# A layer's first RMS norm moved into the stage of the mixer's input projection

## What is computed

```python
def _rms(x, g):
    xf = x.astype(jnp.float32)
    y = xf * lax.rsqrt(jnp.mean(xf * xf, axis=-1, keepdims=True) + EPS)
    return (y * g.astype(jnp.float32)).astype(x.dtype)

def _layer(x, cond, p, ck, cv, cstate):
    mod = jax.nn.silu(cond) @ p['w_mod'] + p['b_mod']
    sh1, sc1, g1, sh2, sc2, g2 = jnp.split(mod, N_MOD, axis=-1)
    h = _rms(x, p['norm1']) * (1.0 + sc1) + sh1
    out, ctx = _token_mixers(h, p, ck, cv, cstate)
    x = x + g1 * out
    ...
```

## Time and profile before

| | |
|---|---|
| median of 3 runs | 5839.04 us (5838.94 to 5841.78) |
| the profiled execution | 5846.38 us, its span 5844.6 us |
| TensorE busy (matmul) | 5424.8 us, 93% of the span |
| TensorE weight loads | 5213.8 us, 89% |
| VectorE | 3252.5 us, 56% |
| ScalarE | 2191.8 us, 38% |
| GpSimd | 2133.7 us, 37% |
| mean granted TensorE clock | 0.966 of 2.4 GHz |

### The profile page before, as it was taken

How to read it: one execution, slowest core, us unless ns; L and a number is a source line. 1 busy time by engine, 2 the same in 40 slices (tenths; PEclk the granted TensorE clock), 3 DMA queues, 4 the chain that set the end, 5 groups by cost and what they waited for, 6 DMA issues and landing times. The chain is left out here.

```text
span 5844.6 us, 118044 instructions
## 1 busy us (share of the span) xinstructions
PE 5424.8 (93%) x47828; PEld 5213.8 (89%) x47828; DVE 3252.5 (56%) x6038; ACT 2191.8 (38%) x2761; POOL 2133.7 (37%) x968
## 2 busy tenths in 40 slices
PE   7977888999999999999989688889999999999999
PEld 3856788999999999999977577889999999999998
DVE  5545648646654156666644564775556522666665
ACT  4433322555555422222233432235555563222221
POOL 0001222656656533343300012236555654433332
PEclk8989999999999999999999899999999999999999
DMA  6100112455555654545411001225555556455443
GB/s 247 58 25 11 62 55 85 143 170 172 178 168 171 210 193 161 169 164 171 142 63 52 17 5 61 87 92 164 168 172 167 180 164 228 166 173 172 162 168 108
DMA packets 303870, 777.73 MB, mean 133 GB/s; under 512 B 23596, under 2 KB 109100, under 8 KB 299368
## 3 DMA queue, kind: packets, MB, share of 16 engines
q1 hardware_dynamic: 303464, 771.94, 39.2%
HBM read 586.52 MB, written 185.34 MB: 132 GB/s over the span
## 5 line engine op out<-in xcount | busy, mean ns | idle before, releaser
L2169 POOL TENSOR_TENSOR ex_v_lo<-ex_v_raw,ex_v_hi 128x1024 fp32r<-128x1024 f32 x256 | 692.1, 2725 | 1071.1 <-ACT ex_v_hi L2075 1071.1
L344 PE MATMUL ex_ps<-tk_h_hi,tk_u_hi 128*128 128x320 f32 x4096 | 968.4, 318 | 43.6 <-POOL tk_u_lo L2157 35.1
L344 PE MATMUL ex_ps<-tk_h_hi,tk_u_lo 128*128 128x320 f32 x4096 | 940.9, 311 | 26.8 <-issue 26.8
L2157 POOL TENSOR_TENSOR tk_u_lo<-tk_u_raw,tk_u_hi 128x1024 fp32r<-128x1024 f32 x256 | 643.4, 2514 | 882.0 <-ACT tk_u_hi L2045 881.7
L344 PE MATMUL ex_ps<-ex_wa_hi,ex_v_hi 128*128 128x320 f32 x4096 | 935.2, 310 | 18.8 <-issue 18.8
L344 PE MATMUL ex_ps<-tk_h_lo,tk_u_hi 128*128 128x320 f32 x4096 | 938.8, 311 | 0.0
L344 PE MATMUL ex_ps<-ex_wa_lo,ex_v_hi 128*128 128x320 f32 x4096 | 934.6, 309 | 0.0
L344 PE MATMUL ex_ps<-ex_wa_hi,ex_v_lo 128*128 128x320 f32 x4096 | 934.5, 309 | 0.0
L2329 DVE TENSOR_TENSOR ex_y<-ex_y,ex_ps 128x640 f32<-128x640 f32 x496 | 405.9, 818 | 671.3 <-PE ex_ps L344 666.5
L344 PEld LDWEIGHTS ex_ps<-tk_h_hi,tk_u_hi 128*128 128x128 f32 x4096 | 682.7, 190 | 45.6 <-POOL tk_u_lo L2157 36.0
L344 PEld LDWEIGHTS ex_ps<-tk_h_hi,tk_u_lo 128*128 128x128 f32 x4096 | 690.8, 189 | 27.5 <-issue 27.5
(11 more groups left out here) (323 smaller groups left out, 7783.2 us busy)
## 6 DMA issues: line engine op xcount, KB each, us to landing
tk_u_raw<-in_expert_u SPq DMA_DIRECT2D x256, 512.0 KB, 4.4
ex_v_raw<-in_expert_v SPq DMA_DIRECT2D x256, 512.0 KB, 3.5
act_spill<-tk_act_e SPq DMA_DIRECT2D x256, 320.0 KB, 2.3
grid_scratch<-tk_grid SPq DMA_DIRECT2D x160, 512.0 KB, 5.7
ex_g<-grid_scratch SPq DMA_DIRECT2D x64, 1280.0 KB, 10.5
x<-in_w_mod_rows SPq DMA_DIRECT2D x192, 256.0 KB, 4.8
ex_a<-act_spill SPq DMA_DIRECT2D x32, 1280.0 KB, 6.3
x<-act_spill SPq DMA_DIRECT2D x32, 1280.0 KB, 6.3
```

The lines of the kernel that those rows point to most:

```text
L344: ins = nc.tensor.matmul(out[:, q, 0:HALF], a, b[:, q * HALF:(q + 1) * HALF], start=(first and n == 0), stop=(last and n == 2))
L2157: nc.gpsimd.tensor_tensor(u_lo[:, at % 2], u_raw[:, at % 3], u_hi[:, at % 2].bitcast(F32), ALU.subtract).then_inc(e["u_split"], 1)
L2169: nc.gpsimd.tensor_tensor(v_lo[h][:, k], v_raw[:, k], v_hi[h][:, k].bitcast(F32), ALU.subtract).then_inc(e["v_split"], 1)
```

## The change

The call of rms_modulate for the first norm goes; its instructions are written into the streams of mixer_input's stage, with the same arithmetic. Its buffers are now parts of rk (h, total and the reciprocal) and of side (sums, wide and the target of the fillers), which the stage uses later for other things. One stage is left where there were two.

On SP nothing is edited: the requests of weights 0 and 1, the constants and the spill of x are the stage's first instructions. On ACT high(0) stands between the squares and the root, high(1) behind the root, then come the eight high parts, then high(2). On DVE low(0) stands between the additions and the mean, low(1) between the reciprocal and the scaling loop, low(2) behind it. On PE the fillers beside the squares stay and those in the scaling loop go; blocks 0 and 1 are made there in first_blocks: in step n PE waits for low part n of the norm, multiplies kb = n for block 0, and kb = n - 3 (BEHIND) for block 1. Block 2 and all later ones are made as before.

```diff
--- before.py
+++ after.py
@@ -350,7 +350,7 @@
 
     order = [Z_AD, Z_WD] + [Z_RKV + 4 + b for b in range(4)] + [Z_RKV + 8 + b for b in range(4)] + \
             [Z_RKV + b for b in range(4)] + [Z_K, 0, 1, 2, 3, Z_V, Z_GD]
-    N = len(order)
+    N, BEHIND = len(order), 3
     FIRST = {name: order.index(n) for name, n in (("k", Z_RKV + 4), ("v", Z_RKV + 8), ("r", Z_RKV), ("qk", Z_K))}
     z, rk = s.z, s.rkv
     value, kmod, kk = s.x[:, 4:8, :], (s.mix[:, 4:8, :], s.x[:, 0:4, :]), s.mix[:, 0:4, :]
@@ -384,11 +384,14 @@
         wide_k, wide_q = z[0:10, Z_V, :], z[0:10, Z_AD, :]
         ps = mem.enter_context(nc.psum_tensor("mi_ps", [P, 2, 2, 512], F32))
         side = mem.enter_context(nc.psum_tensor("mi_side", [P, 2, 2, 512], F32))
+        h, total, inv = rk[:, 0:3, :], rk[:, 3, :], rk[:, 4, 0:TILES]
+        sums, idle, wide = side[:, 0, 0, :], side[:, 0, 1, :], side[:, 1]
 
         names = ["w_in0", "w_in1", "rate_in", "sel_in", "x_out", "hi", "low", "done", "out", "small", "wd_tanh", "rate_done",
                  "rate_tanh", "rate_a", "rate_c", "running", "scanned", "kmod", "conv", "kk_sq", "kk_summed", "kk_ms", "kk_sqrt",
                  "kk_root", "kk_wide", "kk", "kka", "y", "y_summed", "bonus", "bonus_out", "v_turned", "v_taken", "qk_sq",
-                 "qk_summed", "qk_ms", "qk_sqrt", "qk_root", "qk_wide", "qk", "chain"]
+                 "qk_summed", "qk_ms", "qk_sqrt", "qk_root", "qk_wide", "qk", "chain", "x_sq", "x_added", "x_summed", "x_ms", "x_root",
+                 "x_inverse", "x_wide", "x_scaled", "x_high", "x_low"]
         with stage(nc, *["mi_" + n for n in names]) as (block, *sems):
             e = dict(zip(names, sems))
             w_in = (e["w_in0"], e["w_in1"])
@@ -430,11 +433,36 @@
             def _(pe):
                 mm, tr = nc.tensor.matmul, nc.tensor.transpose
 
+                def normed():
+                    for kb in range(KB):
+                        pe.wait_ge(e["x_sq"], kb + 1)
+                        mm(idle[:, 0:HALF], s.ones[:], s.x[:, kb, 0:HALF], start=True, stop=True)
+                    pe.wait_ge(e["x_added"], KB - 1)
+                    for m in range(TILES):
+                        last = mm(sums[:, m:m + 1], total[:, m * P:(m + 1) * P], s.ones[:, 0:1], start=True, stop=True)
+                    last.then_inc(e["x_summed"], 1)
+                    pe.wait_ge(e["x_inverse"], 1)
+                    for m in range(TILES):
+                        out = wide[:, 0, 0:P] if m == 0 else wide[:, 1, (m - 1) * P:m * P]
+                        last = mm(out, inv[:, m:m + 1].broadcast_to([P, P]), s.ident[:], start=True, stop=True)
+                    last.then_inc(e["x_wide"], 1)
+
+                def first_blocks():
+                    pe.wait_ge(e["low"], 2)
+                    for n in range(KB + BEHIND):
+                        if n < KB:
+                            pe.wait_ge(e["x_low"], n + 1)
+                        for u, kb in ((0, n), (1, n - BEHIND)):
+                            if 0 <= kb < KB:
+                                last = matmul_split(nc, ps[:, u], w_hi[:, u, kb], w_lo[:, u, kb], hi[:, kb], lo[:, kb],
+                                                    kb == 0, kb == KB - 1)
+                                if kb == KB - 1:
+                                    last.then_inc(e["done"], 1)
+
                 def project_block(n):
                     u = n % 2
                     pe.wait_ge(e["low"], n + 1)
-                    if n >= 2:
-                        pe.wait_ge(e["out"], n - 1)
+                    pe.wait_ge(e["out"], n - 1)
                     for kb in range(KB):
                         last = matmul_split(nc, ps[:, u], w_hi[:, u, kb], w_lo[:, u, kb], hi[:, kb], lo[:, kb],
                                             kb == 0, kb == KB - 1)
@@ -522,8 +550,11 @@
                         pe.wait_ge(e["qk"], b - 1)
                     widened(side[:, 1 - b % 2], wide_q, root_q, b, 5).then_inc(e["qk_wide"], 1)
 
+                normed()
+                first_blocks()
                 for n in range(N):
-                    project_block(n)
+                    if n >= 2:
+                        project_block(n)
                     if 2 <= n < 10:
                         rates((n - 2) // 4, (n - 2) % 4)
                     if n == 9:
@@ -551,6 +582,12 @@
                         act.wait_ge(e["done"], n - 1)
                     nc.scalar.activation(w_hi[:, n % 2], raw[:, n % 2], ACT.Copy).then_inc(e["hi"], 1)
 
+                def high_part(kb):
+                    act.wait_ge(e["x_scaled"], kb + 1)
+                    for c, a, b in SEGMENTS:
+                        last = nc.scalar.activation(hi[:, kb, a:b], h[:, kb % 3, a:b], ACT.Identity, bias=s.mod[:, kb, c:c + 1])
+                    last.then_inc(e["x_high"], 1)
+
                 def evacuate(n):
                     act.wait_ge(e["done"], n + 1)
                     new = ps[:, n % 2, :, 0:HALF]
@@ -591,11 +628,20 @@
                     act.wait_ge(e["v_turned"], m + 1)
                     nc.scalar.activation(s.v_tok[:, m, :], side[:, 1 - m % 2, 0, :], ACT.Copy).then_inc(e["v_taken"], 1)
 
+                for kb in range(KB):
+                    if kb >= 3:
+                        act.wait_ge(e["x_added"], max(1, kb - 3))
+                    nc.scalar.activation(h[:, kb % 3], s.x[:, kb], ACT.Square).then_inc(e["x_sq"], 1)
                 high(0)
+                act.wait_ge(e["x_ms"], 1)
+                nc.scalar.activation(inv, inv, ACT.Sqrt).then_inc(e["x_root"], 1)
                 high(1)
+                for kb in range(KB):
+                    high_part(kb)
+                high(2)
                 for n in range(N):
                     evacuate(n)
-                    if n + 2 < N:
+                    if 3 <= n + 2 < N:
                         high(n + 2)
                     if n == 1:
                         act.wait_ge(e["out"], 2)
@@ -640,6 +686,21 @@
                     v.tensor_tensor(w_lo[:, n % 2], raw[:, n % 2], w_hi[:, n % 2].bitcast(F32),
                                     ALU.subtract).then_inc(e["low"], 1)
 
+                def scaled(kb):
+                    if kb >= 3:
+                        dve.wait_ge(e["x_low"], kb - 2)
+                    for c, a, b in SEGMENTS:
+                        last = v.scalar_tensor_tensor(h[:, kb % 3, a:b], s.x[:, kb, a:b], s.gain1[:, kb, c:c + 1],
+                                                      wide[:, c, 0:b - a], ALU.mult, ALU.mult)
+                    last.then_inc(e["x_scaled"], 1)
+
+                def low_part(kb):
+                    dve.wait_ge(e["x_high"], kb + 1)
+                    for c, a, b in SEGMENTS:
+                        last = v.scalar_tensor_tensor(lo[:, kb, a:b], h[:, kb % 3, a:b], s.mod[:, kb, c:c + 1],
+                                                      hi[:, kb, a:b].bitcast(F32), ALU.add, ALU.subtract)
+                    last.then_inc(e["x_low"], 1)
+
                 def shifted(zn, j):
                     src, dst = z[:, zn, :], conv_out[zn]
                     for _, a, c in SEGMENTS:
@@ -651,13 +712,28 @@
                 v.tensor_scalar(half0[:, 0:8], s.pvs("a0"), 0.5, None, ALU.mult)
                 v.tensor_scalar(one_ka[:], s.pvs("k_a"), -1.0, 1.0, ALU.mult, ALU.add)
                 v.tensor_scalar(half0[:, 8:16], s.pvs("w0"), 0.5, None, ALU.mult).then_inc(e["small"], 1)
+                for kb in range(1, KB):
+                    dve.wait_ge(e["x_sq"], kb + 1)
+                    v.tensor_tensor(total, h[:, 0] if kb == 1 else total, h[:, kb % 3], ALU.add).then_inc(e["x_added"], 1)
+                    dve.wait_ge(e["x_added"], kb)
                 low(0)
+                dve.wait_ge(e["x_summed"], 1)
+                v.tensor_scalar(inv, sums[:, 0:TILES], 1.0 / D, EPS, ALU.mult, ALU.add).then_inc(e["x_ms"], 1)
+                dve.wait_ge(e["x_root"], 1)
+                v.reciprocal(inv, inv).then_inc(e["x_inverse"], 1)
                 low(1)
+                dve.wait_ge(e["x_wide"], 1)
+                for kb in range(KB):
+                    scaled(kb)
+                    if kb:
+                        low_part(kb - 1)
+                low_part(KB - 1)
+                low(2)
                 for n in range(N):
                     if order[n] in conv_out:
                         dve.wait_ge(e["out"], n + 1)
                         at = link.mark(shifted(order[n], 0))
-                    if n + 2 < N:
+                    if 3 <= n + 2 < N:
                         low(n + 2)
                     if order[n] in conv_out:
                         dve.wait_ge(e["chain"], at)
@@ -2414,7 +2490,6 @@
                 s.rkv = mixers.enter_context(nc.sbuf_tensor("rk", [P, KB, T], F32))
                 with nc.sbuf_tensor("cum", [P, KB, CHUNKS, CHUNK + 1], F32) as cum:
                     with nc.sbuf_tensor("h1_hi", [P, KB, T], F32R) as hi, nc.sbuf_tensor("h1_lo", [P, KB, T], F32R) as lo:
```

(1 more changed line is left out.)

## The result

| | before | after |
|---|---|---|
| median | 5840.41 us (5838.94 to 5843.8, 4 runs) | 5770.34 us (5768.04 to 5781.65, 4 runs) |
| the profiled execution, its span | 5846.38 us, 5844.6 us | 5781.65 us, 5779.5 us |
| mean granted TensorE clock | 0.966 | 0.968 |

The spans differ by 65.1 us. The whole document is about the other half: the two stretches that the change edits give what was forecast, and the rest comes from a place that the change doesn't touch.

What follows compares the result with a forecast made beforehand. TensorE, busy 93% of the span, was taken as the bound, idle between norm and projection and partly at the lower clock. Savings of 17.2 and 16.8 us, together 34.0, gave 5805 us from a 5839.04 median; range 5799 to 5813.

Steps and rivals of the forecast that it cites:

- the Sum: Both layers' stretches: 17.2 and 16.8 us saved, together 34.0, giving 5805 us; all later work only moves earlier.
- (1) to (4): Norm before scaling: 0.86 us boundary goes, early weights have 1.5 us or more cover, high(0) and low(0) are hidden.
- (5): Ahead of the scaling loop: high(1) and low(1) make the loop start 0.5 us later.
- (6): Scaling loop: same instructions in the same order, so each low part ends 0.5 us later than now.
- rival D: Scaling loop: PE's reads of parts being written stretch its rhythm; 5823 us at 3 us a low part; 3%.
- (7): PE in the scaling loop: products replace fillers, block 1 three steps behind; at 2.4 GHz PE ends at 128.0.
- (8): PE clock at the first products: low at first, rising at 120, so ACT takes block 1 at 129.5.
- Rival E: First two blocks: the clock is never in the way; 5802 us; 8%.
- (9): Behind blocks 0 and 1: block 2's weights are split 1.1 us before PE wants them.
- Rival A: First two blocks: clock stays at 1.2 GHz until both are done; 18.5 us saved, 5820.5 us; 8%.
- C: Blocks after the first two: the low clock outlasts them, slower than before; three such blocks a layer give 5855 us; 3%.
- B: Norm: an instruction fetch of ACT or DVE waits for the whole spill of x; 22 us lost, 5827 us; 5%.

Runs made afterwards that it cites:

- The late request: Kernel after with the projection's first weights requested only behind the end of the sum over the features: 5789.02 us, ratio 0.9899.
- the run with fillers: Kernel after with six more filler matmuls between the widening and the first product, and 76 increments at the start: 5781.52 us, ratio 0.9897.

## Why the prediction was wrong, and where it was right

**The step that failed** is in the Sum: "All later work moves by 17 us against the clock's ups and downs; ... so I add 3 us on either side". It took the code outside the two stretches to run as before, only earlier. I priced what each removed instruction costs while it runs, and not that TensorE's stream gets 70 instructions shorter and the experts' loop starts at another place of its 16 KB piece. Worth: 30.7 us by the kernel before with 30 increments, 34.3 us with 186 and their late start, 37.6 us in the profiled pair. The rows of before had it to be read: "issue" 54.1 us in 14 cases is the largest wait of TensorE in the whole run, six of them right behind another, and I had asked the waits only between 94 and 155 us. The signs that I named had a line for this case, "the forecast is wrong if both stretches shrink by 17 us and the span doesn't"; it is the same with the sign turned. The span moved by more than the stretches. None of the rivals covers it.

Without that place the forecast stands. The change alone saves 37.1 us (loop at before's place), 30.3 us (at a place without stalls), 36.7 us (edited stretches of the profiled pair) and 34.8 us (those of the pair with 30 and 100 increments); 34.0 were forecast, between 31.1 and 36.8; the two of these that are differences of medians lie just outside, by less than their runs scatter.

By its steps:

(1) to (4), boundary, requests, high(0), low(0): right. The weights were there (ACT goes from square to high(0) without a wait), the table load starts 0.02 us behind high(0) and ends at 104.55, and the root comes at 105.68, 0.04 us behind the mean square (105.48 + 0.16). So the 1.38 us drain that the Trainium skill states, "ScalarE: Activation LUTs", section "What ACT_TABLE_LOAD costs", is again not seen, as in the earlier trace rows. The late request shows what the cover was worth: some 7 us a layer.

(5) The loop starts 0.34 us late, not 0.5. (6) A low part each 1.84 us from 110.09 to 121.15, and the last at 122.32. Right, and rival D falls: products read these parts and the rhythm doesn't change.

(7) Right: block 1 three steps behind, PE 0.58 us idle ahead of step 3 and then no more.

(8) **Mis-sized.** The clock was low where I had it, and rose at 115.2 instead of 120. Windows of after, which answer to the earlier trace rows:

```profile
102.00:108.40 6.40, 4.69 (x28) 3.51 (x26) 5.16 (x9) 3.69 (x5) 0.00 (x0) 0.99 0.96 409
108.40:115.20 6.80, 3.95 (x13) 3.49 (x14) 6.63 (x15) 3.96 (x8) 0.00 (x0) 0.51 0.40 133
115.20:130.00 14.80, 14.22 (x95) 13.71 (x95) 9.20 (x18) 7.03 (x12) 0.00 (x0) 1.00 0.07 25
```

I had counted the 3.4 to 6.7 us from step 3 on, where work is unbroken; it rose 3.9 us after the first product (111.25), and TensorE's rows show no idle time between the two: at the lower clock the splits of steps 0 to 2 followed each other without a gap up to the rise. The splits that I charged at 1.60 us behind step 3 ran at 0.88. That is 1.3 us a layer: block 1 comes 20.7 us after scaling starts, not 22. Rival E, "the clock is never in the way", is what held in these stretches: its 36.8 us are the 36.7 measured, and the run with fillers has block 1 at the same 20.67 us with the clock up, so with three steps of slack the low clock costs nothing. My charge of 1.4 us a layer for it was the term of (8) that was too large.

(9) Right for BEHIND 3: block 2's weights are ready in time. With BEHIND 0 they are what is late next, by 1.6 us.

Rival A (the clock stays low through both blocks) and C (longer) fall by the third window: 1.00 from 115.2. The rule of the Trainium skill, "TensorE: Matmul & The Clock Gate", section "A second HAM failure mode: psum-queue depth-cycling", would have brought A, and the traces disagree as that of before did: in the run with six fillers TensorE stood 0.47 and 0.64 us between its groups of matmuls and the clock stayed at 1.00. B falls: the spill of x ran under the norm (10.9 us to landing, 11.2 before) and nothing waited for it. What it feared, code that waits behind data, may be a part of the stalls in the experts' loop, where I hadn't looked.

## What to carry to other kernels

An edit that changes the number of instructions ahead of a long hardware loop moves the loop in its 16 KB pieces of code, and that can be worth as much as the edit: ask the waits of the whole run, "issue" above all, for pairs of gaps behind a jump back, and put the loop's start well ahead of the end of a piece. It costs a few idle instructions placed under a wait: here 30 of them took 30.7 us off the unchanged kernel. To judge an edit, compare it at two places of the loop, or the place is judged with it.

## What the runs showed of the hardware

- A jump back of TensorE over a body of 2947 instructions costs 1.2 to 1.8 us every time, and the packet with the 16 KB behind the target's piece starts 3.0 to 5.6 us after that gap begins (1.7 and 1.9 in two of 84 cases), among data transfers that keep the DMA engines busy from 0.8 us on, and is usable after 5.9 to 7.7 (the ends of the second stalls). How much code lies between the loop's start and the end of its piece decides on a second stall: some 8 instructions (6 in the kernel after with 70 increments) gave 3.6 to 5.3 us, some 42 gave 1.3 to 1.9, some 78 and more gave none. The figures 42 and 8 are from the matmuls that ran in between; 78 is 8 and the 70 of the change.
- The other loop of the experts (before L2032) has 790 instructions by the listing and jumps back fourteen times a layer: no packet of this queue and no gap over 0.6 us of TensorE there. So a loop of 790 is kept on the engine, and one of 2947 isn't. Where the border lies no run shows.
- A semaphore increment on TensorE took 0.157 us.
- In the 3.7 us without a matmul ahead of the first product the clock fell from 2.4 to 1.2 GHz, in both layers of seven profiled runs of after and its variants; six filler matmuls in that time held it at 2.4. In the experts' loop it fell behind two of six stalls of 1.3 to 1.9 us, and behind one jump's gap of 1.8 us (after with 256 increments); behind the jumps' gaps of 1.2 to 1.6 us in after it didn't.
